# A fused two-block transformer kernel: ten weight slots instead of nine, half-tile steps in norms and router path, and accumulator banks zeroed in four rounds

## What is computed

```python
def first_block(x, ...):          # layer 0: attention + state space mixer; layer 1: causal pooling mixer
    for layer in range(2):
        h = rmsnorm(x, pre_norm[layer])
        y = even_mixer(h, ...) if layer == 0 else odd_mixer(h, ...)
        x = x + rmsnorm(y, post_norm[layer])
    return x

def second_block(x, ...):
    h = x
    for layer in range(2):
        h = h + hybrid_mixer(rms_norm(h, norm1_g[layer]), w_in[layer], ...)   # retention + HGRN2
        h = h + expert_choice_ffn(rms_norm(h, norm2_g[layer]), w_router[layer], w_gate[layer], w_up[layer], w_down[layer])
    return rms_norm(h, final_norm_g)

def expert_choice_ffn(xn, w_router, w_gate, w_up, w_down):
    affinity = softmax(xn @ w_router)                 # 16 experts
    gate, idx = top_k(affinity.T, 32)                 # each expert chooses 32 tokens
    xe = xn[idx]
    hid = silu(xe @ w_gate) * (xe @ w_up)             # hidden width 1024
    return scatter_add((hid @ w_down) * gate, idx)
```

## Time and profile before

| | us |
|---|---|
| median of 3 runs | 1712.32 |
| lowest, highest | 1712.03, 1713.57 |
| the profiled execution | 1711.37 |
| its span in the trace | 1709.6 |
| PE busy | 1333.4 (78%) |
| VectorE busy | 559.1 (33%) |
| ScalarE busy | 424.6 (25%) |
| GpSimd busy | 136.4 (8%) |
| read from memory | 514.30 MB |

### The profile page before, as it was taken

The page is one execution under the profiler, slowest core; times in us unless marked ns, Lnnn a source line. Parts: engine busy times, 40 slices in busy tenths (PEclk is TensorE's granted clock), DMA queues, the critical chain, the costliest instruction groups (busy, mean ns, idle before and its releaser), DMA issues.

```text
span 1709.6 us, 28214 instructions
## 1 busy us (share of the span) xinstructions
PE 1333.4 (78%) x12496; PEld 923.3 (54%) x12496; DVE 559.1 (33%) x790; ACT 424.6 (25%) x538; POOL 136.4 (8%) x155
## 2 busy tenths in 40 slices
PE   7999889999899987665665666999986666566564
PEld 5688767998798853232322233788843223223232
DVE  8855775455566430000000001485520000000001
ACT  5236334443465311000101011455210101000011
POOL 0120300000304000000000000204000000000000
PEclk9999999999999989798889887999989888888886
DMA  9134243564443699999999999333799999999996
GB/s 326 51 124 148 111 164 114 174 219 149 147 149 124 245 398 426 424 428 425 427 425 427 426 426 411 133 137 133 286 408 425 426 427 424 428 424 428 425 426 264
DMA packets 86148, 516.38 MB, mean 302 GB/s; under 512 B 6336, under 2 KB 6464, under 8 KB 53056
## 3 DMA queue, kind: packets, MB, share of 16 engines
q1 hardware_dynamic: 82576, 509.20, 73.3%
q0 software_dynamic: 992, 3.42, 0.6%
q10 hardware_dynamic: 2512, 2.75, 0.5%
HBM read 514.30 MB, written 1.05 MB: 301 GB/s over the span
## 4 chain that ended last, share of the span: by engine, by line
DMA 47%; PE 39%; DVE 6%; POOL 2%; ACT 2%; issue 2%; SPq 1%; DVEq 0%; ACTq 0%; POOLq 0%
DMA ring<-in_w_down 24%; DMA ring<-in_w_gate 20%; PE dense L1475 8%; PE dense L1477 8%; PE dense L1476 8%; PE bank L1955 3%; DMA ring<-in_w_up 2%; PE dense L1492 2%; PE bank L1980 2%; DMA ring<-in_even_w_in 1%; PE bank L1814 1%; DVE ring_parts L1147 1%; POOL work L655 1%; PE bank L1900 1%; PE dense L1911 1%
## 5 line engine op out<-in xcount | busy, mean ns | idle before, releaser
L1955 PE MATMUL bank<-ring,work 128*32 128x256 f32 x2688 | 203.3, 457 | 143.9 <-DMA ring<-in_w_up 87.7
L1955 PEld LDWEIGHTS bank<-ring,work 128*32 128x32 f32 x2688 | 92.3, 126 | 249.6 <-DMA ring<-in_w_up 108.5
L1147 DVE TENSOR_TENSOR ring_parts<-ring,ring_parts 128x4096 fp32r<-128x4096 f32 (+1 forms) x44 | 184.1, 4194 | 115.8 <-ACT ring_parts L779 115.7
L951 ACT ACTIVATE work<-bank 128x256 f32<-128x256 f32 x32 | 12.3, 384 | 750.5 <-PE bank L1955 750.5
L1407 DVE TENSOR_TENSOR work<-work,bank 128x256 f32<-128x256 f32 x32 | 13.5, 421 | 563.0 <-ACT work L951 563.0
L779 ACT ACTIVATE ring_parts<-ring 128x4096 fp32r<-128x4096 f32 (+1 forms) x45 | 154.1, 3432 | 96.2 <-DMA ring<-in_w_in 40.4
L1955 PE MATMUL bank<-work 128*32 128x256 f32 x1408 | 105.8, 454 | 71.2 <-DMA work<-in_w_up 45.1
L1980 PE MATMUL bank<-ring,work 128*32 128x256 f32 x1344 | 91.8, 419 | 59.6 <-DMA ring<-in_w_down 54.9
L1475 PE MATMUL dense<-xT_parts,ring_parts 128*128 128x256 f32 x448 | 129.5, 289 | 2.7 <-DVE ring_parts L1147 2.7
L1477 PE MATMUL dense<-xT_parts,ring_parts 128*128 128x256 f32 x448 | 126.8, 283 | 0.0
L1955 PEld LDWEIGHTS bank<-work 128*32 128x32 f32 x1408 | 49.9, 127 | 124.8 <-DMA work<-in_w_up 55.7
(11 more groups left out here) (325 smaller groups left out, 2202.5 us busy)
## 6 DMA issues: line engine op xcount, KB each, us to landing
ring<-in_w_gate SPq DMA_DIRECT2D x42, 2048.0 KB, 41.0
ring<-in_w_up SPq DMA_DIRECT2D x42, 2048.0 KB, 41.0
ring<-in_w_down SPq DMA_DIRECT2D x42, 2048.0 KB, 40.8
work<-in_w_gate SPq DMA_DIRECT2D x22, 2048.0 KB, 40.6
work<-in_w_up SPq DMA_DIRECT2D x22, 2048.0 KB, 40.7
work<-in_w_down SPq DMA_DIRECT2D x22, 2048.0 KB, 41.1
ring<-in_w_in SPq DMA_DIRECT2D x18, 2048.0 KB, 8.6
ring<-in_even_w_in SPq DMA_DIRECT2D x10, 2048.0 KB, 10.6
```

Source lines behind the costliest of these rows:

```text
L1147: tt(lo, slot_of(u), hi.bitcast(F32), ALU.subtract).then_inc(lo_done, 1)
L1955: last = mm(WB[0][32 * q:32 * q + 32, 256 * (j % 2):256 * (j % 2) + 256], xeT[:, 4 * (j // 2) + k, :], w[:, k * D + 256 * q:k * D + 256 * ...
```

## The change

It has these parts.

- *Ten slots.* `EXTRA` becomes 4 and `EXTRA_AT` 3584, `TURN_E` 5. `xT` and `work` become one area, `board`, so that the fourth extra slot can reach over `xT`; the small tiles of the expert stage are packed below 3584, and `rgT` and `hgT` move. The extra slots are used where j modulo 10 is 2, 3, 4 or 9. Their first loads wait for different things: j = 4 for `gm_sb` and the first output unit, j = 3 for `rp_ps`, j = 2 for `ho_ps`, j = 9 for the logits (`lg_ps`). SyncE issues j = 2 ahead of the two output units and j = 3 behind them, ahead of j = 0 and 1.
- *Router path.* VectorE adds by halves. PE transposes tile 0 ahead of the last quarter of the last output unit and makes its logits, and half of tile 1's transposes, ahead of that quarter's last three products.
- *Zeros.* The zeros are 512 columns in the split format; one round of four products stands between the logits and the transpose of the probabilities, three rounds behind that transpose.
- *Norms.* The square sums, the scaling, the additions and the transposes of `norm_between` go by halves, and ScalarE makes the high part.
- *Seam and end.* Between the expert stage of layer 1 and layer 2, PE starts the unsplit unit when tile 0 has its gain; tile 1's transposes stand inside the unit, and VectorE makes the high and low parts behind both gains. The output is sent tile by tile.

```diff
-EXTRA, EXTRA_AT = 3, 5632
+EXTRA, EXTRA_AT = 4, 3584
 WHEEL = RING + EXTRA
-TURN_E = 3
+TURN_E = 5
+
+EXTRA_OF = {2: 2, 3: 1, 4: 0, 9: 3}
...
                     elif s >= RING:
-                        sp.wait_ge(gm_sb, 4 * (l + 1))
+                        if s == RING:
+                            sp.wait_ge(gm_sb, 4 * (l + 1))
+                        sp.wait_ge(*((unit_done, OUT2[l] + 1), (rp_ps, RH * (l + 1)), (ho_ps, l + 1), (lg_ps, l + 1))[s - RING])
...
+                load_moe(0, 2)
+                for u in range(OUT2[l], MOE[l]):
+                    load(u)
+                load_moe(0, 3)
                 for j in range(6 * TURN_E):
-                    load_moe(j // 6, j)
+                    if j not in (2, 3):
+                        load_moe(j // 6, j)
...
+                at = 2 * (k - 1)
+                dense_rms = lambda i: rms_halves(i, DP[i], (half_ps, at + i + 1), (tile0_ps, k) if i == 0 else (unit_done, last + 1))
+                sum_rms = lambda i: rms_halves(i, x[:, i, :].rearrange("p (b n) -> p b n", b=2), (sum_half, at + i + 1),
+                                               (x_ready, at + i + 1))
+                dense_rms(0)
+                sum_rms(0)
+                dense_rms(1)
+                gain_high(0, at)
+                sum_rms(1)
+                gain_high(1, at)
+
+            def rms_halves(i, of, first, second):
+
+                act.wait_ge(*first)
+                own.link(s.activation(xs[:, i, 0:512], of[:, 0, :], ACT.Square, accum_out=stat[:, 7, 0:1]))
+                own.go(s.activation(stat[:, 7, 1:2], stat[:, 7, 0:1], ACT.Identity, scale=1.0 / D, bias=eps[:]))
+                act.wait_ge(*second)
+                own.link(s.activation(xs[:, i, 512:1024], of[:, 1, :], ACT.Square, accum_out=ssq[:, i:i + 1]))
+                s.activation(std[:, i:i + 1], ssq[:, i:i + 1], ACT.Sqrt, scale=1.0 / D, bias=stat[:, 7, 1:2]).then_inc(std_ready, 1)
+
+            def gain_high(i, at):
+
+                for half in range(2):
+                    c = slice(4 * half, 4 * half + 4)
+                    act.wait_ge(gained, 2 * (at + i) + half + 1)
+                    s.activation(xT_r[:, c, i * P:(i + 1) * P], xs[:].rearrange("p i (c s) -> p c i s", c=DC)[:, c, i, :],
+                                 ACT.Copy).then_inc(gain_hi, 1)
...
-                ahead_of[0] = [[], [] if l else [at(transpose_x, 1)], [tile_in_xT], []]
+                ahead_of[0] = [[], [at(transpose_x, 1)], [full_rows if l else tile_in_xT], []]
...
                     rows_unit(OUT2[l] + n, [[t[:, c, :] for c in chunks] for t in (m_hi, m_lo)], n == 0, n == 1,
-                              [[], [], [at(mix_transposes, 0)], []] if n == 0 else ())
-
-                pe.wait_ge(router_in, 32)
-                for i in range(NT):
-                    pe.wait_ge(x_ready, 5 + 6 * l + i)
-                    transpose_rows(x, i)
-                    tile_in_xT()
-                    for k in range(DC):
-                        last = mm(WB[0][:, NE * i:NE * i + NE], xT[:, k, i * P:(i + 1) * P], wr[:, l, k, :], start=k == 0,
-                                  stop=k == DC - 1)
-                last.then_inc(lg_ps, 1)
+                              [[], [], [at(mix_transposes, 0)], []] if n == 0 else [[], [], [], [first_rows]],
+                              [[], [], [], [first_logits]] if n else ())
+                rows_half(1, 1)
+                logits(1, 0)
+                logits(1, 1).then_inc(lg_ps, 1)
+
+                pe.wait_ge(zero_set, l + 2)
+                yb = [DP[r // 2][:, r % 2, :] for r in range(4)]
+
+                def zero(rounds):
+
+                    for _ in range(rounds):
+                        for r in range(4):
+                            last = mm(yb[r], zeros[:, 0:P], zeros, start=True, stop=True)
+                    return last
+
+                zero(1).then_inc(ge_ps, 1)
                 pe.wait_ge(aff_sb, l + 1)
                 for i in range(NT):
                     last = tr(WB[1][0:NE, i * P:(i + 1) * P], aff[:, i, :], ident)
                 last.then_inc(aff_ps, 1)
+                zero(3).then_inc(gt_ps, 1)
...
-            sp.wait_ge(final_done, NT)
-            sp.dma_start(out.rearrange("(i p) n -> p i n", p=P), xs[:]).then_inc(out_sent, 16)
-            sp.wait_ge(out_sent, 16)
+            for i in range(NT):
+                sp.wait_ge(final_done, i + 1)
+                sp.dma_start(out[i * P:(i + 1) * P, :], xs[:, i, :]).then_inc(out_sent, 16)
+            sp.wait_ge(out_sent, 16 * NT)
```

More of the change, by code:

```diff
@@ L553, in _ @@
             for l in range(2):
-                for u in range(FIRST2[l], MOE[l]):
+                for u in range(FIRST2[l], OUT2[l]):
                     load(u)
@@ L980, in normalise @@
                 inverse(i)
-                ts(xs[:, i, :], x[:, i, :], rstd[:, i:i + 1], None, ALU.mult).then_inc(xs_ready, 1)
+                for b in range(2):
+                    half = slice(512 * b, 512 * b + 512)
+                    ts(xs[:, i, half], x[:, i, half], rstd[:, i:i + 1], None, ALU.mult).then_inc(xs_ready, 1)
             def gain_out(i, name, low=None):
@@ L998, in gain_out @@
                        WB[2 * i + half][:].rearrange("p (c s) -> p c s", c=4), g, ALU.mult).then_inc(xT_ready, 1)
+                for half in range(2 if low is not None else 0):
+                    count["hi"] += 1
+                    dve.wait_ge(gain_hi, count["hi"])
+                    c = slice(4 * half, 4 * half + 4)
+                    tt(low[:, c, i, :], xs[:].rearrange("p i (c s) -> p c i s", c=DC)[:, c, i, :],
+                       xT_r[:, c, i * P:(i + 1) * P].bitcast(F32), ALU.subtract).then_inc(xT_ready, 1)
             def norm_between(k, name):
@@ L1511, in t_unit, with rows_unit @@
                 last.then_inc(unit_done, 1)
-            def rows_unit(u, act_T, first, last_unit, slots=()):
+            def rows_unit(u, act_T, first, last_unit, slots=(), late=()):
                 w = slot_of(u, u in SPLIT)
@@ L1520, in rows_unit @@
                         for k in range(4):
+                            if k == 3:
+                                ahead(late, 2 * i + n)
                             if u in SPLIT:
@@ L1868, in mix_transposes, with rows_half, first_rows, logits @@
                         last.then_inc(gm_ps, 1)
+                def rows_half(i, half):
+                    pe.wait_ge((x_half, x_ready)[half], ((1 + 2 * l, 5 + 6 * l)[half]) + i)
+                    for c in range(4):
+                        last = tr(WB[2 * i + half][:, c * P:(c + 1) * P], x[:, i, (4 * half + c) * P:(4 * half + c + 1) * P], ident)
+                    last.then_inc(xt_ps, 1)
+                def first_rows():
+                    for half in range(2):
+                        rows_half(0, half)
+                def logits(i, half):
+                    count["xT"] += 1
+                    pe.wait_ge(xT_ready, count["xT"])
+                    for k in range(4 * half, 4 * half + 4):
+                        last = mm(WB[0][:, NE * i:NE * i + NE], xT[:, k, i * P:(i + 1) * P], wr[:, l, k, :], start=k == 0,
+                                  stop=k == DC - 1)
+                    return last
+                def first_logits():
+                    for half in range(2):
+                        logits(0, half)
+                    rows_half(1, 0)
                 read_out = (1, 2, 4, 6, 7, 8, 9, 10, 11)
```

191 lines of the change are left out of this document (114 added, 77 removed).

## The result

The changed kernel takes **1704.1 us** (median of 5 runs, 1702.28 to 1705.62), the kernel before 1713.57 in the same comparison (1712.03 to 1716.78): ratio **0.9948**, 95% interval 0.9929 to 0.9968. It is 9.5 us faster; 20 were forecast, and the time lies outside the range. The profiled execution has a span of 1702.2 us where the earlier trace rows belong to one of 1709.6.

A forecast was written before the change was run, and what follows sets the result against it. The kernel was taken to alternate between expert stages bound by reading weights and mixers bound by PE and its helpers. Terms -9.8 -2.2 -1.2 -1.8 -2.9 -0.7 -1.2 sum to -19.8: 1692 us, range 1686.5 to 1700.

The forecast's parts named there:

- Part 1: Expert stages: with a tenth slot filled early, 86 instead of 87 loads follow the first release; -4.9 us a layer, -9.8.
- rival C: Expert stages: the tenth slot is not in by the release, losing up to 4.9 us a layer; 1697 to 1701, chance 0.06.
- Rival D: Expert stages: ten loads in flight lower the stream's rate, deciding from 2.3%; at 4% 1725 us, chance 0.03.
- Part 2: Router path, last output unit to logits: reordered transposes and logits bring logits earlier, -2.2 us in layer 1, -1.2 in layer 2.
- The zeros: Between logits and expert stage: the new zero products cost nothing at full clock, 0.1 and 0.3 us at half.
- Rival A: Between zeros and experts: 2.5 us of PE idleness drops the clock, +4.4 us a layer, net +3.2 twice; 1698, chance 0.12.
- Part 3: Norms between the first block's layers: work in halves and ScalarE's cast save -1.8 us at the first, -2.9 at the second.
- norm 1: First norm between layers: unit 15's high and low parts become what is late next; -1.8 us, bounds -0.5 to -3.0.
- Norm 2: Second norm between layers: PE's awaited chain starts 3.3 us earlier, less 0.4 for a table load; -2.9, bounds -1.0 to -3.4.
- rival B: Norms: hops between ScalarE and VectorE eat the halves, so the norms give nothing; +4.7 us, 1696.5, chance 0.09.
- Part 4: Seam between expert stage 1 and layer 2: PE starts the float32 unit earlier; -0.7 us, bounds -1.6 to +0.5.
- Part 5: Output at the kernel's end: sent in two DMAs, so the last carries half; -1.2 us, bounds 0 to -1.3.

The follow-up runs named there:

- run 2: The changed kernel with nine slots and three experts a turn, all its other edits kept: 1701.39 us, ratio 0.994.
- run 5: The changed kernel with the tenth slot used once a layer and a three-expert loop running from half an expert to half an expert: 1694.12 us, ratio 0.9895.
- run 3: The changed kernel with nine slots and six experts a turn, all its other edits kept: 1711.86 us, ratio 1.0.
- run 6: The kernel of run 5 with the accumulator banks set to zero once instead of four times: 1693.88 us, ratio 0.9882.
- run 1: The kernel before, nine slots kept, with TensorE's and SyncE's expert loops at six experts a turn instead of three: 1724.65 us, ratio 1.0073.
- run 7: The kernel before with TensorE's sixteen experts written out straight, SyncE's loop kept: 1726.29 us, ratio 1.0071.
- run 8: The kernel before with eight slots and four experts a turn: 1734.49 us, ratio 1.0124.
- run 4: The changed kernel with the tenth slot used once a layer, three experts a turn and four straight experts outside the loop: 1696.57 us, ratio 0.9907.

## Why the prediction missed, step by step

**The step that failed is Part 1, the tenth slot.** Its basis was the sentence "in a plateau only bytes count", and the edit TURN_E = 5, which the tenth slot brings with it, has no term in the sum, not even a bound. Forecast -9.8; measured +1.95 and +0.84 us in the two plateaus (table), 12.6 us off. The slot itself is worth what was said: between run 2 and run 5 the plateaus become 4.77 and 3.94 shorter, 8.7 in all. The loop took that back and more: between run 2 and run 3, which differ in it alone, the plateaus become 5.6 and 5.3 longer, 10.9; between run 5 and the changed kernel 7.5 and 5.7, 13.2. From release to last landing the three are 9.6, 8.9 and 12.0. The sentences on how the ten slots are filled held, but the margin was half a microsecond and not three: the engines moved 213 GB/s in 618 to 619, and the release came at 619.0. So rival C, a tenth slot that isn't in by the release, was close and did not come.

**Rival D** had the right place and the wrong cause: a loss that grows inside the plateau. It looked at the rate, which would have had to fall by 2.3% to decide. The weights moved in 700 to 1040 went from 144.96 to 143.93 MB, 0.7% less or 2.4 us of the 340, and 0.41 MB of code came in beside them. A mean over sixteen engines shows only part of the loss, since half of the shares were on time and TensorE waits for the last.

**Part 2, router path**: forecast -2.2 and -1.2; measured -4.1 and -2.8. The logits were ready at 604.8, 3.8 earlier than at 610.04, net of the norms. PE's timeline of the changed kernel:

```profile
598.41 1.85 PE L1980 MATMUL bank<-wr,board 128*128 128x16 f32 x16
...
602.83 1.96 PE L1980 MATMUL bank<-wr,board 128*128 128x16 f32 x16
```

The second 16 pieces took 1.96 us where the earlier trace rows have 3.60. The mis-sized term is the clock: a middle between full and half was taken, and it was at full until the logits were through; it fell at 606.0, where it had fallen at 603.1 before. For full clock the prediction has -3.0, but its own terms (603.4 + 0.6 + 1.45 + 1.1 to 1.2) add up to 606.6 and not to 606.8 to 607.1, so -3.4; the other 0.4 is the unit's end, at 601.45, some 0.5 earlier than priced (net of the norms). Part of the 4.1 is bad luck of the kernel before, which has 35.60, while 34.63 and 34.39 occur with the same path: against the mean of the four the path gained 3.5.

**The zeros**: cost nothing, as forecast. That they give something, up to 2 us, was in the text only as its opposite. **Rival A** had the clock fall from 2.5 us of idleness and priced it at 4.4 us a layer. Its sign, half clock in the gather, did show, in layer 2 of the changed kernel, where the clock was at half from 1247.7 to 1251.2 after PE had been idle for 1.27 us; in layer 1, after 1.55, it stayed full. But the gather took 2.03 us at half, as at full, and the path was 31.73 us long against 31.49. Even run 6, at half until 623.1, lost 2.0 and not 4.4. The price was too high, and idleness alone doesn't tell when the clock falls.

**Part 3, norms**: norm 1 forecast -1.8, measured -1.3, in all six profiles but one within 0.1 of it. What was late next was named rightly (unit 15's high and low part), but the gain was taken for all of the chain: VectorE's low part waited for ScalarE's high part and started at 265.34 where the earlier trace rows have 264.93, only 0.2 us earlier when the 0.64 are taken off that this execution was late already, and PE had to wait until 269.91. PE's and VectorE's timelines of the changed kernel:

```profile
269.91 0.47 PE L1562 MATMUL dense<-ring_parts,board_parts 128*128 128x512 f32 x1 [1.46 <-DVE ring_parts L1211]
```

```profile
265.34 8.76 DVE L1211 TENSOR_TENSOR ring_parts<-ring,ring_parts 128x4096 fp32r<-128x4096 f32 x2 [2.82 <-ACT ring_parts L832]
```

Norm 2 forecast -2.9; the profiled pair shows -0.8, the means of four and six profiles -2.8 (37.30 to 34.53). The pair misleads, since the clock falls there, at a different point and for a different time in every execution: for 3.4 us in all in the profile that the earlier trace rows come from, 6.8 in the changed kernel, 10.2 or 10.3 in runs 1, 7 and 8, and not at all in run 4, which has the shortest norm 2. So the earlier trace rows come from the luckiest of the four. Windows 446 to 451, the kernel before, then the changed one:

```profile
446.00:451.00 5.00, 2.26 (x11) 1.63 (x10) 4.85 (x2) 4.53 (x3) 0.33 (x1) 1.00 0.36 99
```

```profile
446.00:451.00 5.00, 3.20 (x20) 3.23 (x21) 5.00 (x2) 1.62 (x2) 3.23 (x1) 0.80 0.77 261
```

So rival B, norms that give nothing, did not come: by the means they gave 4.1 of the 4.7.

**Part 4, seam**: forecast -0.7, measured +0.5 in the pair and -0.1 in the means, within its bounds. **Part 5, output**: forecast -1.2, measured -2.3 in the pair and -1.5 in the means, both outside its bounds (0 to -1.3); the tail varies by about 1 us from one execution to the next, and no run tells the rest apart.

**The account**: measured, by means where there are several, -1.3 (norm 1), -2.8 (norm 2), -3.5 and -2.8 (router paths), -0.1 (seam), -1.5 (tail) make -12.0, where -10.0 was forecast; the plateaus give +2.8 where -9.8 was forecast. Together -9.2; the runs say -9.5. (The profiled pair alone gives -8.1, and 0.6 us lost ahead of the first norm; its spans differ by 7.4.) So the small parts were right to 2 us in sum, which is in part luck: the router paths gave 2.9 more than priced, norms and seam 1.2 less, the output 0.3 more. The largest part carried the whole miss. The 0.66 for the forecast rested on a mechanism that was thought through for bytes and for slots and never for what else its edit changed.

## What to carry to other kernels

When an edit changes how far a loop is written out, cost the code as a transfer: count its instructions against what the engine keeps, and look at the line of the instruction queue before and after. In this stage, bound by DMA, some 400 KB of code cost 4.4 to 6.2 us where their bytes take 1.0, since they set back half of the shares only and a transfer is done when its slowest share is. A resource that is worth something once (here the tenth slot, in the filling) need not join the rotation: used once and left, it kept its 4.8 and 4.9 us a layer and cost no code.

## What the runs showed of the hardware that was not expected

- TensorE's code is read in 16 KB packets of 1.1 us each, 1.8 to an expert of this kernel where it runs straight (run 7); a body of three experts is read once, one of four, five or six again and again (q8: 55 packets a run against 103 to 108).
- A code packet sets back one of eight shares of a load, in turn, and the other eight not at all. Summed over the shares, the lag behind the eight early ones grows by 1.4 to 1.6 us a packet in the changed kernel and in runs 1, 3, 7 and 8. In runs 3 and 8 and the changed kernel 13 of the 16 gaps between two steps of the spread are eight packets long; in runs 1 and 7 a second share steps ahead at times. Why it is 1.5 us and not the packet's 1.1, and why these eight, stays open.
- Run 2's plateaus are 0.8 and 0.9 us shorter than those of the kernel before, with the same loop and the same slots. It isn't the stream: from release to last landing they take 432.3 and 433.4 us, against 431.9 and 433.3. The difference lies in TensorE's work behind the last landing (2.0 us against 3.2 in stage 1, where the clock was at full in run 2 and fell at 1057.1 in the kernel before).
- Not tried: ten slots in rotation with a short loop, which this way of addressing the slots can't express. That the standing tenth slot has a cost of its own beside its loop's is thus not excluded: from release to last landing the changed kernel lost 12.0 us against run 5, run 3 only 8.9 against run 2. Part of it is the last step of the spread, at 1038 in stage 1 of the changed kernel, which run 3 doesn't reach.
